# Hyena long convolutions: the odd frequencies of the way back paired as f and 1024-f, and the odd products taken first on the way there

## The reference

```
def fft_long_conv(u, spec, skip):
    L = u.shape[1]
    uf = jnp.fft.rfft(u.astype(jnp.float32), n=2 * L, axis=1)
    y = jnp.fft.irfft(uf * spec[None], n=2 * L, axis=1)[:, :L]
    return (y + u.astype(jnp.float32) * skip.astype(jnp.float32)).astype(u.dtype)
def hyena_sequence(u3, short_w, short_b, spec, skip):
    ...
    for o in range(C_ORDER):
        z = parts[o + 1] * fft_long_conv(z, spec[:, o], skip[o])
```

## Time and profile before

| | us |
|---|---|
| median of 3 runs | 3578.36 (3573.93 to 3579.75) |
| the profiled execution | 3573.62 |
| its span, first to last instruction | 3571.8 |
| PE busy | 3383.8 |
| DVE busy | 1790.1 |
| ACT busy | 1300.8 |
| POOL busy | 676.2 |

### The profile page before, as it was taken

How to read it: one execution, slowest core, us unless ns; L and a number is a source line. 1 busy time by engine, 2 the same in 40 slices (tenths; PEclk the granted TensorE clock), 3 DMA queues, 4 the chain that set the end, 5 groups by cost and what they waited for, 6 DMA issues and landing times. The chain is left out here.

```text
span 3571.8 us, 39788 instructions
## 1 busy us (share of the span) xinstructions
PE 3383.8 (95%) x15662; PEld 2465.9 (69%) x15662; DVE 1790.1 (50%) x2260; ACT 1300.8 (36%) x2098; POOL 676.2 (19%) x380
## 2 busy tenths in 40 slices
PE   6989999998999999999999999979988999999997
PEld 3646444555888888888988777543444888888886
DVE  3233544432555544644775433683464555445444
ACT  4333344445543333422553232622111543333322
POOL 0000477666341001200301000100000320003001
PEclk8999999999999999999999999989999999999999
DMA  8753523330443323433553210103411442323322
GB/s 334 271 202 100 173 63 74 74 82 16 144 153 117 113 95 103 134 100 99 172 189 131 88 50 27 42 37 126 156 42 50 139 135 95 100 95 118 124 95 100
DMA packets 133801, 407.19 MB, mean 114 GB/s; under 512 B 24169, under 2 KB 38281, under 8 KB 129136
## 3 DMA queue, kind: packets, MB, share of 16 engines
q1 hardware_dynamic: 133616, 404.65, 34.2%
HBM read 345.59 MB, written 58.92 MB: 113 GB/s over the span
## 5 line engine op out<-in xcount | busy, mean ns | idle before, releaser
L1543 ACT ACTIVATE w_high<-w_raw 128x1024 fp32r<-128x1024 f32 x372 | 392.4, 1055 | 580.7 <-PE psum L1506 472.1
L1636 DVE TENSOR_TENSOR w_low<-w_raw,w_high 128x1024 fp32r<-128x1024 f32 x372 | 469.3, 1262 | 123.7 <-ACT w_high L1543 122.5
L1506 PE MATMUL psum<-hid_high,w_high 128*128 128x512 f32 (+1 forms) x1280 | 473.3, 370 | 12.5 <-DVE hid_low L1720 10.2
L1489 PE MATMUL psum<-h_high,w_high 128*128 128x512 f32 (+1 forms) x1280 | 474.8, 371 | 0.4 <-DVE w_low L1636 0.4
L1506 PE MATMUL psum<-hid_low,w_high 128*128 128x512 f32 (+1 forms) x1280 | 471.5, 368 | 0.0
L1506 PE MATMUL psum<-hid_high,w_low 128*128 128x512 f32 (+1 forms) x1280 | 471.4, 368 | 0.0
L1489 PE MATMUL psum<-h_high,w_low 128*128 128x512 f32 (+1 forms) x1280 | 470.9, 368 | 0.0
L1489 PE MATMUL psum<-h_low,w_high 128*128 128x512 f32 (+1 forms) x1280 | 470.9, 368 | 0.0
L1742 POOL TENSOR_TENSOR squares_then_rstd_of_out<-squares_then_rstd_of_out,square_out 128x512 f32<-128x512 f32 (+1 forms) x70 | 104.7, 1495 | 1287.7 <-ACT square_out L1558 1287.7
L1253 POOL TENSOR_TENSOR probs_added<-probs_added,probs_turned 128x1024 f32<-128x1024 f32 x128 | 305.8, 2389 | 68.2 <-ACT probs_turned L1186 55.7
L1224 DVE TENSOR_REDUCE row_max<-psum 128x1 f32<-128x1280 f32 x120 | 179.0, 1492 | 229.2 <-PE psum L1124 137.2
(11 more groups left out here) (410 smaller groups left out, 5488.5 us busy)
## 6 DMA issues: line engine op xcount, KB each, us to landing
w_raw<-in_ff_w_dram SPq DMA_DIRECT2D x320, 512.0 KB, 3.5
ada_ring<-in_ada_w_dram SPq DMA_DIRECT2D x24, 2048.0 KB, 9.3
w_raw<-in_w_out_dram SPq DMA_DIRECT2D x40, 512.0 KB, 3.4
stream_in<-scratch_x SPq DMA_DIRECT2D x32, 256.0 KB, 3.9
scratch_spectra<-spectrum_out SPq DMA_DIRECT2D x32, 256.0 KB, 2.0
filter_ring<-scratch_spectra SPq DMA_DIRECT2D x16, 512.0 KB, 4.5
w_raw<-in_w_hy_dram SPq DMA_DIRECT2D x12, 512.0 KB, 3.9
scratch_hyena<-mixed SPq DMA_DIRECT2D x12, 512.0 KB, 2.7
```

The costliest lines, as they stand in the source:

```text
L1489: mm = pe.matmul(bank[:, 0:n], x[:, i % SLOTS, k, :], y[:, k, a:a + n], start=(k == 0 and m == 0), stop=(k == KT - 1 and m == 2))
L1506: mm = pe.matmul(bank[:, 0:n], x[:, i % SLOTS, 2 * k + half, :], y[:, k, 0:n], start=(k == 0 and m == 0), stop=(k == HT - 1 and m == 2))
L1543: act.activation(w_hi[:, i % SLOTS], raw[:, i % 2], ACT.Copy).then_inc(w_rounded, 1)
L1636: dve.tensor_tensor(w_lo[:, i % SLOTS], raw[:, i % 2], w_hi[:, i % SLOTS], ALU.subtract).then_inc(w_split, 1)
```

## The change

*Way back, odd frequencies.* For odd frequency f and its partner 1024-f the cosines (and the sines) are equal up to a sign that alternates with the token. So the partners' sum gives the tokens of one parity and their difference those of the other. After the spectral products of an odd tile of the upper half (i = 2, 3), DVE now writes them to a new tile `other` and makes differences and sums with the partner tile of the lower half (8 more instructions of 128x512 in each order, with their own semaphore `paired`). TensorE then multiplies, for each channel tile, cosine and sine, token parity, 2 frequency tiles deep and 256 tokens wide. The results of a bank lie in two halves by parity; DVE writes and reads its other operand (L2715, L2720) with step 2 instead.

*Order of the tokens.* So that the upper frequencies stand as partners, the table of odd frequencies is stored with its upper half reversed; and the folded tokens are taken in steps of 2 (even ones, then odd ones), by the transposes and, in the filters' stage, by the tap products. The filters' spectra are otherwise computed as before.

*Order of the work.* The forward products begin with the odd tiles (0, 2, 1, 3), the sine part first, which needs only the turned tiles of s = 0 and one row; the even tiles follow. ACT puts that row in place after its sixth copy. The filter tiles are loaded in the new order. On the way back channel tile 0 takes its odd products first, and the wait for all of `yv` stands only ahead of its even ones. `back_even` holds four tables instead of two (1 MB instead of 0.5), `back_odd` half of before (1 MB instead of 2).

```diff
-                            at = jt * P + jt // 2
+                            at = jt % 2 + (jt // 2) * (HALF + 1)
...
-                                mm = pe.transpose(g.ps[:, n_turn % 2, ct * P:(ct + 1) * P], fold[:, s, ct, at:at + P], g.ident[:])
+                                mm = pe.transpose(g.ps[:, n_turn % 2, ct * P:(ct + 1) * P], fold[:, s, ct, at:at + HALF - 1:2], g.ident[:])
...
+        tiles = [(1, i) for i in TILE_ORDER] + [(0, i) for i in range(FT)]
...
+                    for n, (parity, i) in enumerate(tiles):
+                        w = o * 2 * FT + n
+                        if n >= 2:
+                            pe.wait_ge(mult, 4 * (w - 1))
+                        if n == FT:
+                            pe.wait_ge(even_folded, 8 * (o + 1))
+                            pe.wait_ge(mid_out, 4 * (o + 1))
+                        for kind in (1, 0):
+                            form, which, cols = even_or_odd(2 * parity + kind, i)
+                            if n == 0:
+                                pe.wait_ge(turned_out, 2 * FT * o + FT * (2 - kind))
+                                pe.wait_ge(mid_out, 4 * o + 3 - kind)
...
+                    def back_odd_products(v, ct, cs, sin_bank, cos_bank):
+                        if ct == 0:
+                            pe.wait_ge(paired, 8 * (o + 1))
+                        for bank, kind in ((cos_bank, 0), (sin_bank, 1)):
+                            for half in range(2):
+                                for i in range(2):
+                                    mm = pe.matmul(g.ps[:, bank, half * HALF:(half + 1) * HALF], yv[:, 2 + kind, 2 * half + i, cs], back_odd[:, kind, half, i, :], start=(i == 0), stop=(i == 1))
+                        mm.then_inc(inverse_odd, 1)
...
-                        for bank, part in ((cos_bank, 2), (sin_bank, 3)):
-                            for i in range(FT):
-                                mm = pe.matmul(g.ps[:, bank, :], yv[:, part, i, cs], back_odd[:, part - 2, i, :], start=(i == 0), stop=(i == FT - 1))
+                        if ct == 0:
+                            back_odd_products(v, ct, cs, sin_bank, cos_bank)
+                            back_even_products(v, ct, cs, e_bank, f_bank)
+                        else:
+                            back_even_products(v, ct, cs, e_bank, f_bank)
+                            back_odd_products(v, ct, cs, sin_bank, cos_bank)
...
+                            if s == 1 and jt == 2:
+                                act.wait_ge(even_folded, 8 * o + 2)
+                                act.activation(tim[0:1, 0, 0, :], g.ps[0:1, 2, :], ACT.Copy).then_inc(mid_out, 1)
...
+                        second = parity and i >= 2
+                        if second and o + i > 2:
+                            dve.wait_ge(paired, 8 * o + 4 * (i - 2))
+                        for kind, op in enumerate((ALU.subtract, ALU.add)):
+                            into = other[:, kind, :] if second else yv[:, 2 * parity + kind, i, :]
+                            dve.tensor_tensor(into, pr[:, 2 * kind, :], pr[:, 2 * kind + 1, :], op).then_inc(combined, 1)
+                        if second:
+                            dve.wait_ge(combined, 2 * (w + 1))
+                            for kind in range(2):
+                                dve.tensor_tensor(yv[:, 2 + kind, i, :], yv[:, 2 + kind, i - 2, :], other[:, kind, :], ALU.subtract).then_inc(paired, 1)
+                            dve.wait_ge(paired, 8 * o + 4 * (i - 2) + 2)
+                            for kind in range(2):
+                                dve.tensor_tensor(yv[:, 2 + kind, i - 2, :], yv[:, 2 + kind, i - 2, :], other[:, kind, :], ALU.add).then_inc(paired, 1)
...
-                        dve.tensor_tensor(s[:, 1:WIDE], s[:, 1:WIDE], g.ps[:, sin_bank, :], ALU.add)
+                        dve.tensor_tensor(by_step(s[:, 1:WIDE]), by_step(s[:, 1:WIDE]), by_half(g.ps[:, sin_bank, :]), ALU.add).then_inc(added, 1)
```

More of the change, by code:

```diff
@@ L2383, in spectrum @@
                         for jt in range(2):
-                            pe.matmul(out[0:1], f.alt_col[:], even[o][:, 0, jt, :], start=(jt == 0), stop=False)
+                            pe.matmul(out[0:1], f.alt_col[:, jt + 1:jt + 2], even[o][:, 0, jt, :], start=(jt == 0), stop=False)
                         mm = pe.matmul(out[0:1], f.alt_row[:, 0:1], mid_sum[:, o, :], start=False, stop=True)
@@ L2529, in long_convs @@
         tm = f.gate[:, 2:4, :]
+        other = tile(nc, mem, "output_spectrum_other", [P, 2, W_HY])
         FOLDS = 6
+        tiles = [(1, i) for i in TILE_ORDER] + [(0, i) for i in range(FT)]
+        by_step = lambda x: x.rearrange("p (i t) -> p t i", t=2)
+        by_half = lambda x: x.rearrange("p (t i) -> p t i", t=2)
         with nc.Block() as block:
@@ L2544, in _ @@
                             sp.wait_ge(mult, 4 * (w - 2))
-                        sp.dma_start(h[:, w % 3], filters[n // FT, n % FT]).then_inc(h_in[w % 3], 16)
+                        sp.dma_start(h[:, w % 3], filters[tiles[n]]).then_inc(h_in[w % 3], 16)
                         if w == 2:
@@ L2574, in _ @@
                             mm.then_inc(turned, 1)
                             n_turn += 1
-                    n = 0
-                    for parity in range(2):
-                        for i in range(FT):
[L2580 to L2598, removed]
@@ new lines, in _ @@
+                    for n, (parity, i) in enumerate(tiles):
[7 more added lines that the diff above has]
+                            form, which, cols = even_or_odd(2 * parity + kind, i)
+                            out = g.ps[:, 3 + 2 * (n % 2) + kind, :]
+                            if n == 0:
+                                pe.wait_ge(turned_out, 2 * FT * o + FT * (2 - kind))
+                                pe.wait_ge(mid_out, 4 * o + 3 - kind)
+                            if form == "odd":
+                                for jt in range(FT):
+                                    mm = pe.matmul(out, odd_tab[:, which, jt, cols], tim[:, 1 - which, jt, :], start=(jt == 0), stop=(jt == FT - 1))
+                            else:
+                                for jt in range(2):
+                                    mm = pe.matmul(out, even_tab[:, which, jt, cols], even[which][jt], start=(jt == 0), stop=(jt == 1 and which > 0))
+                                if which == 0:
+                                    mm = pe.matmul(out, alt_row[:, 0:P], mid, start=False, stop=True)
+                        mm.then_inc(product, 1)
@@ L2603, in _ @@
                     pe.wait_ge(back_in, 32)
-                    pe.wait_ge(combined, 4 * FT * (o + 1))
-                    pe.wait_ge(last_made, o + 1)
                     for ct in range(CT):
@@ L2909, in hyena_tables @@
     a["dft_odd"] = np.ascontiguousarray(np.stack([tiles(cos_odd), tiles(sin_odd)], axis=1).astype(f32))
-    l = np.arange(FOLD)[:, None]
-    a["dft_back_odd"] = np.ascontiguousarray(np.stack([tiles(np.cos(angle(l)).T), tiles(np.sin(angle(l + 1)).T)], axis=1).astype(f32))
+    l, m = np.arange(FOLD)[:, None], np.arange(HALF)[None, :]
+    cos_back, sin_back = np.cos(angle(l)).T, np.sin(angle(l + 1)).T
+    by_half = lambda x: np.stack([x[:, h::2].reshape(2, P, HALF).transpose(1, 0, 2) for h in range(2)], axis=1)
+    a["dft_back_odd"] = np.ascontiguousarray(np.stack([by_half(cos_back), by_half(sin_back)], axis=1).astype(f32))
     j = np.arange(HALF)[:, None]
```

94 lines of the change are left out of this document (45 added, 49 removed).

## The result

| | before | after |
|---|---|---|
| median of 4 runs, us | 3576.28 (3573.93 to 3579.75) | 3529.22 (3528.03 to 3531.79) |
| the profiled execution, us | 3573.62 | 3529.59 |
| `long_convs`, first turn to the last product of DVE | 234.0 | 192.3 |

The ratio is 0.9875 [0.9863, 0.9888]: faster by 47 us. A second measurement of the two kernels gave 3533.43 (3530.13 to 3533.89) against 3574.87, ratio 0.9886 [0.9873, 0.99]. The forecast was 3537 us, with a range of 3528 to 3548, and a stage near 193: the first median lies close to the lower edge of the range.

The account below looks back on a forecast made before the run. TensorE, busy 95% of the span, was taken to bound the kernel, with pauses and clock falls in each order. Gains of 19.8 and 21.4 us, 41.2 together, off the 3578.36 median gave 3537 us, range 3528 to 3548.

Parts of the forecast that it names:

- The mechanism and the sum: Over the long-convolution stage: gains of 19.8 us in order 0 and 21.4 in order 1, together 41.2.
- The start: Head of each order: first products at S + 7.5 (order 1: 7.65), S the first turn; pause and clock price go, 4.4 us.
- half of the added DVE work on the path: Forward products: of 5.2 us added to DVE an order, 2.6 hidden and 2.6 on the path; DVE ends at S + 58.1.
- No fall of the clock: Ahead of the way back's even products: TensorE pauses only some 0.4 us, so the clock stays at full.
- a clock that falls as before: Rival: all four falls of the clock in the stage stay, 8.7 us come back, 3546 us; chance 12%.
- Odd products back: Way back on TensorE: half the columns, same instruction count, so 3.5 us a channel tile instead of 6.97.
- the bound of no gain: Way back: the odd products gain nothing at all if the weight load sets the pace.
- DVE beside POOL in order 0: Way back: DVE sets the pace at 8.6 us a channel tile, 7.6 undisturbed plus 1.0 from POOL; end at S + 98.7.
- Order 1: Second order, without folding: TensorE sets the way back's pace, 8.5 us a tile; end at S + 94.1, gain 21.4.
- Halved products that don't shorten: Rival: the way back's odd products stay as long, 7 x 3.5 us return on the path, 3561 us; chance 4%.
- a clock that stays low: Rival: 1.2 GHz from the stretch DVE paces to an order's end, 52 us an order, 104 in all, 3641; chance 3%.
- Steps of 2: Stride-2 fp32 operands on DVE and in the turns cost nothing; rival at half rate, 11 us, 3548 us, chance 10%.

Follow-up runs that it names:

- e5: Changed kernel with the first forward product again waiting for all second folds and all middle-token rows; 3541.71 us, ratio 0.99, stage 201.4 us.
- e8: Changed kernel with DVE's eight pairing instructions of an order cut to one column; 3530.31 us, ratio 0.9869, stage 191.7 us.
- e11: Changed kernel with four more 128x512 subtractions on DVE behind each of the two pairings; 3539.34 us, ratio 0.9906, stage 199.1 us.
- e1: Changed kernel with the old order of forward products and way back, keeping the partners' pairing and halved products; 3554.17 us, ratio 0.9949, stage 216.2 us.
- e4: Changed kernel with channel tile 0 taking its even products first on the way back; 3545.30 us, ratio 0.9917, stage 203.6 us.
- e6: Changed kernel with POOL's two additions on the way back cut to one column; 3530.36 us, ratio 0.987, stage 190.5 us.
- e10: Changed kernel with the turns reading 128 tokens in a row instead of every second one; 3528.59 us (one run), stage 192.1 us.

## Why the prediction was right, and where it wasn't

**The mechanism and the sum.** 41.2 us were summed for the stage and 41.8 and 41.5 came (19.8 and 21.4 by order, against 20.8 and 21.0). The median of the first measurement fell by 47, that of the second by 41.4; the 5.6 between them is not explained by the stage, whose length repeats within 0.3. That the first median came out 8 us under the forecast is thus mostly not the change. The forecast was counted down from 3578.36, a median of three; the same kernel's later medians are 3573.78 to 3576.80, which takes off 1.6 to 4.6. The stage gave 0.3 to 0.6 more than forecast. The rest is spread outside the stage: the two changed profiles reached it 3.6 us apart. That 3529 still fell within the range, by 1 us, is owed to its width and not to the sum.

**The start.** S + 7.5 and 7.65 forecast; 7.48 and 7.70 came. e5 prices the pause and its clock at 8.9 for both orders, 4.4 an order in the forecast.

**Forward products: half of the added DVE work on the path.** This step failed, by size and not in its time. Forecast: 2.6 us of the pairing on the path of each order, DVE sets the end, S + 58.1, and TensorE pauses 0.4 ahead of the even products. By e8 the pairing costs 0.3 to 0.4 us an order. Measured: no pause ahead of the even products, which start at S + 58.0. DVE's second upper tile takes 6.38 (2549.38 to 2555.76), not 6.5, and `yv` is complete at 2571.98 = S + 57.8. TensorE's forward products end at S + 54.4, not 54.2, and this delay is itself a wait for DVE: 0.37 us at the last even tile, for banks (the PEld row under e8); without the pairing they end at S + 54.2, as forecast. The forecast had both ends (57.7 for TensorE, 58.1 for DVE) and still called 2.6 us "on the path"; by its own numbers it was 0.4. That size came, but among the forward products and not ahead of the way back. e11 shows the other side: 2.4 us beyond this cost 2.4, and 4.3 where the clock falls.

**No fall of the clock.** Right at all four places where the kernel before had a pause (two in each order), and the rival of a clock that falls as before is out. e1, e4 and e5 bring falls back one by one: behind pauses of 4.49, 3.45 and 2.59 us, at 4.2, 3.3 and 1.8 us each.

**Odd products back.** 3.5 us a tile forecast, 3.56 came (2582.33 to 2585.89); the bound of no gain is out. (The even products of a tile are 24 instructions and not 22; nothing hangs on it.)

**DVE beside POOL in order 0.** 8.6 a tile forecast, 8.26, 8.24 and 8.36 came (L2742 at 2580.21, 2588.47, then 2605.07 for two tiles on). The other term of the sum that was mis-sized: POOL costs 0.8 to 0.9 a tile (e6: 7.45 without it) and not 1.0 on top of 7.6. With 0.9 less over the three tiles, order 0 ends at S + 97.7 and not 98.7.

The Trainium skill ("SBUF — State Buffer", Terms) has the loser of the shared port pair block in full. As the forecast priced this rule, at the whole length of both additions, the tile would have been 9.4. The rows agree that each side holds the other, but the hold on DVE is shorter than a row of POOL: beside L2682 and L2683 (2592.93, 1.70 where it took 0.72 undisturbed) DVE's L2760 takes 1.63 instead of 1.22 and L2262 0.83 instead of 0.41 (as at 2586.94). So DVE is held twice a tile, about 0.4 us each time. The two together only happen to come near the length of one POOL addition.

**Order 1.** 94.1 forecast, 94.5 came: TensorE sets the pace as said, 8.6 a tile.

**The other rivals.** Halved products that don't shorten, and a clock that stays low, are out by the rows above: 3.56 a tile, 1.00 in all four windows.

**Steps of 2.** On DVE L2742 takes 0.67 to 0.69 us, L2715 took 0.69: nothing, as taken. For the turns it isn't quite so: 210 ns instead of 162 for a weight load (e10). By the Trainium skill's note on cachelines ("SBUF — State Buffer", section "Door 1") a step of up to four fp32 elements is free. The rows of DVE agree, the weight loads of the turns don't.

**What stays open.** Why the time ahead of the stage moves by up to 6 us between profiles of the same work; why in e11 the same pause is followed by a fall in one order and not in the other (of the columns shown, the DMA share beside it differs, 0.29 and 0.79, and it was not tried). No kernel tried is faster than the changed one by more than its spread and computes the same.

## What to carry to other kernels

Work that is moved to an engine with slack costs nothing only where another engine's work stands behind it: here all but 0.7 of 10 us of DVE instructions are hidden when TensorE has products that need no result of theirs, and without that (e1) they cost a pause and then the clock. When a sum says that an engine sets the end, compute the end of the second one too; the price of an edit is the distance between them and not the length of the added work. And a pause ahead of dense matmuls is priced with the slow stretch behind it, which cost nearly as much as the pause in e1 and e4. Buffers are a second path for such work: DVE here delays TensorE by the banks that it frees late, before it delays it by its results.

## What was not expected of the hardware

A stationary fp32 operand of a transpose, read in steps of 2, loads in 210 ns instead of 162 (e10), while DVE takes no longer for such operands (0.67 to 0.69 us for L2742, 0.69 for L2715). A pause of 2.20 us was followed by 1.2 GHz in one order and by 2.4 GHz in the other, at a difference of 1.9 us, and 1.83 us was enough for a fall in the kernel before. DVE and POOL slow each other by turns: L2263 took 0.94 instead of 0.41 while L2683 took 0.90, and in the tile before it was L2683 that took 1.70.
